# Block one of a two-block network: small products of the linear attention and of the norms moved between the passes of the projection tiles

## The reference

```python
h = rmsnorm(x, attn_norm_g);  proj = h @ w_in          # split into the parts below
gla_q, gla_k, gla_v, gla_r, gla_lr, mb_q, mb_k, mb_v, mem_q = split(proj)
g_log = log_sigmoid(gla_lr @ w_gla_gk + b_gla_gk) / 16
o_gla = rmsnorm(gla_chunked(gla_q, gla_k, gla_v, g_log)) * silu(gla_r)
o_moba = moba_attention(rmsnorm(mb_q), rmsnorm(mb_k), mb_v)      # softmax attention, per head
o_mem = memory_attention(rmsnorm(mem_q), rmsnorm(mem_k), mem_v)  # keys, values from mem
x = x + concat(o_gla, o_moba, o_mem) @ w_out

def gla_chunked(q, k, v, g):     # chunks of 64 tokens
    cum = cumsum(g, inside each chunk);  last = cum[end of chunk]
    q_dec, k_inv, k_end = q * exp(cum), k * exp(-cum), k * exp(last - cum)
    o_intra = tril(q_dec @ k_inv.T) @ v            # inside a chunk
    d_state = k_end.T @ v                          # what a chunk adds to the state
    state = running sum of d_state, decayed by exp(last)
    return o_intra + q_dec @ state
```

## Time and profile before

| | us |
|---|---|
| median of 3 runs before | 1747.68 (1746.02 to 1751.62) |
| the profiled execution, device time | 1748.58 |
| its span, first to last instruction | 1746.8 |
| PE busy | 1694.1 (97%) |
| stages 0 to 15 of the first block, in the span | about 44 to 204 |

### The profile page before, as it was taken

One profiled execution on the slowest core, in us unless ns is written; L12 is line 12 of the kernel. 1 busy time (PEld: TensorE's weight loads), 2 busy tenths in 40 slices (PEclk: granted clock), 3 DMA queues, 4 the chain that ended last, 5 costly groups with the idle time before them and its releaser, 6 DMA issues.

```text
span 1746.8 us, 20029 instructions
## 1 busy us (share of the span) xinstructions
PE 1694.1 (97%) x8132; PEld 1177.0 (67%) x8132; DVE 698.7 (40%) x1121; ACT 604.7 (35%) x785; POOL 577.6 (33%) x279
## 2 busy tenths in 40 slices
PE   8999999999999999999999989999999999999996
PEld 5677765344434444437788867777788888888885
DVE  5774445233333333348651013333344421212146
ACT  5665435101000100124751245554333432323232
POOL 2332134222022202014344435555444343434441
PEclk9999999999999999999999999999999999999998
DMA  5121174899999999983212111112242222222301
GB/s 213 61 85 48 39 280 159 343 419 421 421 420 421 421 421 421 421 329 121 87 59 96 49 49 48 50 49 86 78 175 97 97 96 97 96 97 96 134 12 48
DMA packets 79068, 312.74 MB, mean 179 GB/s; under 512 B 3168, under 2 KB 6656, under 8 KB 54272
## 3 DMA queue, kind: packets, MB, share of 16 engines
q1 hardware_dynamic: 78704, 310.38, 45.6%
q0 software_dynamic: 272, 1.05, 0.2%
HBM read 307.22 MB, written 4.19 MB: 178 GB/s over the span
## 4 chain that ended last, share of the span: by engine, by line
PE 88%; DVE 7%; ACT 3%; issue 1%; POOL 1%; DMA 0%; DVEq 0%; SPq 0%; ACTq 0%
PE ps L905 44%; PE ps L1275 13%; PE ps L955 7%; PE ps L1299 6%; PE ps L1228 4%; PE ps L903 2%; PE ps L1418 2%; PE ps L1244 2%; PE ps L1245 1%; PE ps L1407 1%; PE ps L1455 1%; PE ps L1392 1%; ACT sb_slot L1501 1%; DVE sb_xT L2329 1%; DVE sb_h_low L2048 1%
## 5 line engine op out<-in xcount | busy, mean ns | idle before, releaser
L839 POOL TENSOR_TENSOR sb_w_parts<-sb_slot,sb_w_parts 128x2048 fp32r<-128x2048 f32 x59 | 274.9, 4659 | 379.1 <-ACT sb_w_parts L1501 379.1
L905 PE MATMUL ps<-sb_h_high,sb_w_parts 128*128 128x512 f32 x1120 | 268.4, 392 | 0.0
L905 PEld LDWEIGHTS ps<-sb_h_high,sb_w_parts 128*128 128x128 f32 x1120 | 210.2, 188 | 46.9 <-issue 3.1
L1501 ACT ACTIVATE sb_w_parts<-sb_slot 128x2048 fp32r<-128x2048 f32 x59 | 112.8, 1913 | 195.7 <-PE ps L905 186.7
L1275 PE MATMUL ps<-sb_slot,sb_hT 128*64 128x512 f32 x768 | 171.1, 595 | 0.0
L905 PE MATMUL ps<-sb_hidden_high,sb_w_parts 128*128 128x512 f32 x704 | 165.0, 389 | 0.0
L905 PEld LDWEIGHTS ps<-sb_hidden_high,sb_w_parts 128*128 128x128 f32 x704 | 132.2, 188 | 27.4
L803 POOL TENSOR_TENSOR sb_tile_parts<-sb_slot,sb_tile_parts 128x1024 fp32r<-128x1024 f32 x32 | 78.4, 2449 | 189.8 <-ACT sb_tile_parts L1501 189.8
L905 PE MATMUL ps<-sb_h_low,sb_w_parts 128*128 128x512 f32 x560 | 138.0, 389 | 0.0
L1275 PEld LDWEIGHTS ps<-sb_slot,sb_hT 128*64 128x64 f32 x768 | 53.6, 137 | 106.2 <-issue 106.2
L825 POOL TENSOR_SCALAR sb_chosen<-sb_cst,sb_small 128x256 fp32r<-128x256 f32 x28 | 25.3, 921 | 293.5 <-PE ps L1228 293.5
(11 more groups left out here) (339 smaller groups left out, 2639.9 us busy)
## 6 DMA issues: line engine op xcount, KB each, us to landing
sb_slot<-w_up SPq DMA_DIRECT2D x24, 2048.0 KB, 14.9
sb_slot<-w_gate SPq DMA_DIRECT2D x24, 2048.0 KB, 14.9
sb_slot<-w_down SPq DMA_DIRECT2D x21, 2048.0 KB, 15.8
sb_slot<-w_in SPq DMA_DIRECT2D x14, 2048.0 KB, 7.9
sb_R<-w_down SPq DMA_DIRECT2D x11, 2048.0 KB, 15.3
sb_slot<-tiles SPq DMA_DIRECT2D x32, 512.0 KB, 3.3
sb_R<-w_gate SPq DMA_DIRECT2D x8, 2048.0 KB, 14.4
sb_R<-w_up SPq DMA_DIRECT2D x8, 2048.0 KB, 15.4
```

What stands on the lines that cost most here:

```text
L839: nc.gpsimd.tensor_tensor(low, raw_part(g), high.bitcast(F32), ALU.subtract).then_inc(w_low, 1)
L905: ins = nc.tensor.matmul(o, w[:, k, at:at + P], h[:, k, :], start=first, stop=last)
L1501: return nc.scalar.activation(dst, src, f, **kw)
```

## The change

In a stage with one filling tile, PE does two of its three passes (a new step `passes`), then the posts and those steps of `late` that are named in `inner`, and then the tile's last pass. With two filling tiles these steps stand between the tiles. The posts and inner steps thereby stand ahead of `evict` and `norm_rows` in the list, for all engines. A tile's job number is given out only after the posts and inner steps, though PE begins the tile before them. DVE's running sum of `decay` becomes a step of its own, `decay_sum`, at stage 3 (it was in stage 2) and stage 6 (it was in stage 4); ACT's part of `decay` stays. Nothing is added or left out.

```diff
-    late = {0: ["mem_acc"], 1: ["mem_sum"], 2: [("decay", 0)], 4: [("decay", 1)], 5: [("decay_qk", 0)], 8: [("turn_keys", 0), ("intra", 0)],
+    late = {0: ["mem_acc"], 1: ["mem_sum"], 2: [("decay", 0)], 3: [("decay_sum", 0)], 4: [("decay", 1)], 5: [("decay_qk", 0)], 6: [("decay_sum", 1)], 8: [("turn_keys", 0), ("intra", 0)],
+    inner = ("turn_keys", "intra", "chunk_state", "gla_sum", "gla_row", "gla_scale", "gla_norm")
+
+    def middle(i):
+        if i == 0:
+            post("mk", 1)
+        elif fills[i - 1][0] != "gla_out":
+            for f in fills[i - 1]:
+                post(*f)
+        for e in late.get(i, ()):
+            if e[0] in inner:
+                gla(*e)
...
             if fills[i][0] == "gla_out":
                 gla(*fills[i])
+                step("norm_rows", i)
+                middle(i)
             else:
-                for f in fills[i]:
-                    tile(*f)
+                if len(fills[i]) == 1:
+                    split_to(TILES1.index(fills[i][0]) + 1)
+                    step("passes", *fills[i][0])
+                else:
+                    tile(*fills[i][0])
+                middle(i)
+                tile(*fills[i][-1])
                 for f in fills[i]:
                     step("evict", *f)
-            step("norm_rows", i)
-            if i == 0:
-                post("mk", 1)
-            elif fills[i - 1][0] != "gla_out":
-                for f in fills[i - 1]:
-                    post(*f)
+                step("norm_rows", i)
             for e in late.get(i, ()):
-                gla(*((e,) if type(e) is str else e))
+                if e[0] not in inner:
+                    gla(*((e,) if type(e) is str else e))
...
+                if kind == "passes":
+                    tile(*arg, range(KD), True, True, ((0, 0), (1, 0)))
+                    begun.add(arg)
+                elif kind == "tile" and arg in begun:
+                    tile(*arg, range(KD), True, True, ((0, 1),))
```

More of the change, by code:

```diff
@@ L985, in norm_sum @@
                 nc.tensor.matmul(ps_[:, 7, :], C("ones"), acc, start=True, stop=True).then_inc(summed, 1)
-            pending = []
+            pending, begun = [], set()
             for st in steps:
                 kind, arg = st[0], st[1:]
-                if kind == "tile":
+                if kind == "passes":
[3 more added lines that the diff above has]
+                    tile(*arg, range(KD), True, True, ((0, 1),))
+                elif kind == "tile":
                     if arg[0] == "out":
@@ L2179, in _ @@
                     ins.then_inc(p_ready, 1)
-                elif kind == "decay":
+                elif kind == "decay_sum":
                     pr = arg[0]
```

## The result

| | before | after |
|---|---|---|
| median, us | 1747.39 (1746.02 to 1751.62, 5 runs) | 1770.06 (1769.39 to 1772.45, 5 runs) |
| span of the profiled execution | 1746.8 | 1768.2 |

The ratio is 1.0127 (95% interval 1.0113 to 1.0142): 22.7 us slower. The direction and the mechanism were forecast, the size was not: 1770.1 lies outside the range of 1752 to 1766, and far from 1759.5.

The account below looks back on a forecast made before the run. PE, busy 97% of the span, was taken as the bound, so only its idle stretches and clock could move the time. Gains, bank waits and clock falls summed to +12.8, rounded to +12: 1759.7 us, range 1752 to 1766.

Parts of the forecast that it names:

- The gains of stages 7, 10 and 14: Old PE waits there covered by the tile's last pass: -1.22, -0.93 and -1.03 us.
- the bank waits of stages 9, 11, 12 and 13: PE tiles gq 1, gv 2, gv 3 and r 0 wait for banks ACT frees: 1.8, 2.6, 4.9 and 2.4 us.
- the cover's: A tile's last pass, 8 matmuls of about 1.9 us, put where PE waited for a bank or product.
- the upper bound of stage 6: Longest wait given for tile gv 0: 5.5 us, from scores freed 11.4 us after the tile before.
- the chain: Stage 6, from the end of tile cq 1 to its scores freed: 10.2 us, PE there after 5.8, waiting 4.4.
- After such a wait I count one episode of low clock, +1.3, as in stage 4 before: Stage 6: one fall of PE's clock behind the 4.4 us wait, +1.3 us.
- I charge the two waits that are longer than the one that fell, and leave open those of 1.8, 2.4 and 2.6: Clock falls charged only behind the new waits of stages 6 and 12, +1.3 us each.
- the wait of stage 1: PE waits some 3 us at rowsum, 1.03 before, as DVE takes headsum's reciprocal first; stage 2 starts 1.9 late.
- The third rival: Clock falls after all five new waits: 1763.6 us, or 1767 with stage 2's delay kept; chance 0.17.
- The rule that I weighed: Waits recurring between short bursts of matmuls bring the lower clock back every time; all five new waits would pay.
- product 0.48: Stage 6: link of the chain after the reciprocal and before the eviction, taken as 0.48 us.
- Together -1.6: Stages 0 to 4: stage 2 late, but stage 4's 2.16 us stall and low clock go; bounds -3.5 and +1.9.

Follow-up runs that it names:

- e4_sum_alone: The kernel before with only DVE's running sums of the decays one step later, at stages 3 and 6: 1742.56 us (ratio to before 0.9974).
- e16_all_spin: The changed kernel with idle matmuls in bank 7 ahead of all six PE waits of 1.8 us and more: 1764.17 us (ratio to before 1.0097).
- e11_not_stage6: The changed kernel, but in stage 6 the row sums and value turn stand behind the tile as before: 1767.78 us (ratio to before 1.0111).
- e15_no_sum: The changed kernel with the running sums of the decays back in stages 2 and 4: 1780.78 us (ratio to before 1.0187).
- e1_ring: The changed kernel with PSUM banks dealt out in the order in which PE begins its jobs: 1757.46 us (ratio to before 1.0057).
- e12_mixed: The changed kernel with banks in PE's order of begin, and ACT and DVE taking moved work behind eviction and norm_rows in stages 0 to 7: 1748.87 us.
- e10_not_stage1: The changed kernel, but in stage 1 the row sums stand behind the tile as before: 1772.18 us (ratio to before 1.0141).
- e14_sum_spin: The kernel before with the later running sums, and two idle matmuls instead of one at mem_sum in stage 1: 1742.84 us (ratio to before 0.9975).
- e8_ring_stage12: The kernel before with the later running sums, work inside the tile in stage 12 alone, and banks in PE's order of begin: 1743.16 us.

## Why the prediction was right or wrong

The starts of the stages in the two traces, against the terms of the sum (the first line is all up to the start of stage 5):

| stage | before | after | measured | predicted |
|---|---|---|---|---|
| 0 to 4 | to 97.80 | to 99.58 | +1.8 | -1.6 |
| 5 | to 109.74 | to 111.08 | -0.4 | 0 |
| 6 | to 118.84 | to 129.14 | +9.0 | +5.7 |
| 7 | to 129.25 | to 138.24 | -1.3 | -1.2 |
| 8 | to 138.93 | to 148.79 | +0.9 | 0 |
| 9 | to 148.13 | to 160.21 | +2.2 | +1.8 |
| 10 | to 155.95 | to 167.06 | -1.0 | -0.9 |
| 11 | to 166.68 | to 180.70 | +2.9 | +2.6 |
| 12 | to 177.66 | to 195.90 | +4.2 | +5.0 |
| 13 | to 187.57 | to 210.05 | +4.2 | +2.4 |
| 14 | to 196.28 | to 217.65 | -1.1 | -1.0 |

**Right: the waits.** The gains of stages 7, 10 and 14 and the bank waits of stages 9, 11, 12 and 13 (1.87, 2.55, 3.84, 2.42, forecast 1.8, 2.6, 4.9, 2.4) came as worked out, each with the named releaser; that of stage 12 is shorter because `row_neg` took 0.16 us there and met no POOL operation, and stage 8 waited 0.50 us where nothing was forecast. That the gain of stage 7 is the cover's is not shown, since its wait also goes with the later running sums alone (e4_sum_alone). Of idle time alone the sum had +11.5 us, and the windows show +13.5. The shift is passed on whole behind stage 15. (By its own terms the upper bound of stage 6 is 11.4 - 5.8 = 5.6 us and not 5.5, and the chain has ten links and not eleven; the sum does not change.)

**Wrong, the larger part: the clock.** The sum had +1.3 us net for it (-1.3 in stage 4, +1.3 each in stages 6 and 12); the windows show +7.9, which is 6.6 of the 8.6 us between the sum of 12.8 and the trace's 21.4, and e16_all_spin gives 5.9 of it back. Three sentences failed. "After such a wait I count one episode of low clock, +1.3, as in stage 4 before": in stage 6 the sixteen matmuls took 6.65 us, 2.65 too many. "I charge the two waits that are longer than the one that fell, and leave open those of 1.8, 2.4 and 2.6": the wait of 2.42 us in stage 13 cost 1.55, and in e11_not_stage6 those of 1.87 and 2.55 cost as much. And the wait of stage 1, which I had put at some 3 us, longer than the 2.16 that brought the fall before, got no charge at all; its slow matmuls cost 0.9 (1.84 us for row sums that take 0.95 elsewhere) and 1.7 (3.76 for 2.03). The third rival, "the clock falls after all five new waits", gave 1763.6 to 1767 with a chance of 0.17 and was the nearest. The rule that I weighed for it stands in the Trainium skill, page TensorE: Matmul & The Clock Gate, section HAM oscillation, where waits of 3 to 5 us between short bursts of matmuls bring the lower clock back every time. I had stretched it to shorter waits. In the changed kernel all three waits of 3 us and more (3.20, 3.84 and 5.36 us) brought the fall, and of the three shorter ones (1.87, 2.42 and 2.55 us) one did. So four of six fell, and a threshold read from the one row of 2.16 us was no guide.

**Wrong, the smaller part: stage 6.** The term "product 0.48" is the link that failed: 1.86 us beside POOL, 1.4 of the 1.6 us by which the chain was longer. I had seen that effect in stage 12 and charged it there, where it did not come, and not here. With the 0.82 us ahead of `values` the stage idles 6.2 us instead of 4.4.

**Wrong by its clock: stages 0 to 4.** The term "Together -1.6" measured +1.8. Stage 2 starts 4.8 us late and not the 1.9 forecast; the wait of stage 1 came as forecast (3.20 us for 3), and what failed is its clock, above. From stage 2 to stage 5 some 3.0 us come back, where 3.5 were forecast. That PE waits 1.21 us in stage 4, as forecast (1.1), is in part luck: PE came there about 3 us later than reckoned, and so did the eviction that it waits for (89.4 and not 86.3), 1.3 us of it by the product that took 1.79 us and not 0.48.

The term also took the running sums for a small help. e15_no_sum shows that without them the changed kernel would lose 10.7 us more, e4_sum_alone that by themselves they give 5.4. Measured against e4_sum_alone the work inside the tiles costs 27.5 us, not 22.7.

**What the loss is made of.** Shown: the numbering (12.6 us, e1_ring); in stages 0 to 7 the order on DVE and ACT (8.6 us more, once the numbering is right, e12_mixed). From 1748.9 to 1742.6 about 6 us remain. The traces show 4.8 of them by the start of stage 15: 1.3 by the start of stage 8, and 3.6 in the second half, all in stage 11, with a wait of 1.62 us and slow matmuls behind it. What splitting a tile costs by itself was not isolated; by rows of e12_mixed and e4_sum_alone, a split stage without a wait is 0 to 0.3 us longer than an unsplit one (9.10 for 9.10 us in stage 6, 9.97 for 9.67 in stage 8). I had entered it as nothing.

That e10_not_stage1 is slower than the changed kernel (2 us in the medians, 1.4 at the start of stage 15) is clock by its rows: it starts stage 7 1.0 us earlier, but the sixteen matmuls behind the waits of 2.55 and 3.84 us, which are the same, take 5.54 and 6.43 us and not 4.00 and 5.54. Why the clock falls so there is open.

**What the idea is worth.** In the best form of the whole that was run (e12_mixed) the work inside the tiles is no faster than the kernel before, and it costs some 6 us against e4_sum_alone. Of all that was run, only the kernels with the later running sums and at most one split stage (e4_sum_alone, e14_sum_spin, e8_ring_stage12) are faster than before. Not run: e12_mixed with its wait of stage 11 filled or removed, and the changed numbering with ACT and DVE behind everywhere.

## What to carry to other kernels

When a job is put inside another, look at what its sequence number decides: here the tile took its number at its end but its bank at its beginning, and waited for work of its own stage. Cover on the engine that waits (PE) must not be paid with delay on the engine that it waits for: 4.1 us of norm work put ahead of an eviction on DVE made PE wait 3.2 us in stage 1, more than a pass of matmuls (1.9 us) covers. And where waits are added, price the clock as a term of its own, by the busy time of the same matmuls in two windows, with a range that holds a fall behind every wait; fill such waits with idle matmuls before anything else is judged by them.

## What the runs showed of the hardware that was not expected

- The granted clock does not follow the length of a wait: it stayed up behind 2.55 us in the changed kernel and fell behind 2.42 us in the same execution, and behind 1.87 us in e11_not_stage6. A fall costs 1.5 us over sixteen matmuls of 128x512 (5.53 for 4.00), around the 5.36 us wait 2.65.
- It does not even need a wait of that kind. In e4_sum_alone it is low just behind a wait of 1.02 us (0.76 from 59 to 66 us). In the kernel before it fell where PE had waited for nothing since 190.49 us and did small matmuls just before (the sums of `gla_sum`, sixteen of one column each):

```profile
204.41 1.95 PE L1150 MATMUL ps<-sb_cst,sb_slot 128*128 128x1 f32 x16
206.21 5.52 PE L955 MATMUL ps<-sb_h_high,sb_tile_parts 128*128 128x512 f32 x16
```

- Idle matmuls, two for each count and some 0.44 us from start to start (twelve in 5.42 us ahead of the tile of stage 6), in a bank that nobody reads, kept the granted clock at 1.00 through all stages of the profiled execution of e16_all_spin and gave back 5.9 us of 22.7.
- Operations of DVE on two SBUF operands stretch when they begin while a POOL subtraction of 128x1024 is running. From 40 to 240 us of the 18 traces, the product of 128x256 took 0.48 or 0.49 us in all 14 places without POOL beside it, and 1.75 to 2.40 us in all 21 where it began during a subtraction, ending 0.28 or 0.29 us behind it each time. The eviction of 128x512, which reads PSUM, took 0.69 us beside POOL too (16 places; 0.67 to 0.69 in 200 others), and a reduction of 128x1024, on one SBUF operand, its 1.22 us.
